# An encoder trunk of two layers: latent and neighbourhood attention heads in turns instead of one kind after the other

## The reference

```python
def even_mixer(h, w_in0, g_q, g_kv, w_uq, w_ukv, rpb, w_out0):
    u = h @ w_in0
    q_lat, kv_lat, k_rope, na_q, na_k, na_v, gate = jnp.split(u, ...)
    o_mla = mla(q_lat, kv_lat, k_rope, g_q, g_kv, w_uq, w_ukv)     # 8 heads, 512 x 512 scores each
    o_na = neighbourhood_attn(na_q, na_k, na_v, rpb)               # 8 heads, a window on an 8 x 64 grid, with a bias table
    o = jnp.concatenate([o_mla, o_na], axis=-1) * jax.nn.silu(gate)
    return o @ w_out0
```

## Time and profile before

| | |
|---|---|
| median of 3 runs | 1521.56 us (1518.37 to 1523.8) |
| profiled execution, device time | 1518.78 us |
| its span | 1517.0 us |
| PE busy | 1468.3 us (97%) |
| DVE busy | 849.7 us (56%) |
| ACT busy | 678.4 us (45%) |
| POOL busy | 345.4 us (23%) |

### The profile page before, as it was taken

One profiled execution on the slowest core, in us unless ns is written; L12 is line 12 of the kernel. 1 busy time (PEld: TensorE's weight loads), 2 busy tenths in 40 slices (PEclk: granted clock), 3 DMA queues, 4 the chain that ended last, 5 costly groups with the idle time before them and its releaser, 6 DMA issues.

```text
span 1517.0 us, 18952 instructions
## 1 busy us (share of the span) xinstructions
PE 1468.3 (97%) x7200; PEld 1119.7 (74%) x7200; DVE 849.7 (56%) x1523; ACT 678.4 (45%) x1170; POOL 345.4 (23%) x441
## 2 busy tenths in 40 slices
PE   8999999999999999999999999999999999999996
PEld 4777665678777787788887887567867778787885
DVE  4523345655887517785444345565688651789423
ACT  3323436654433435544544343674443353555333
POOL 0001123431200023765210002342120002376311
PEclk9999999999999999999999999999999999999998
DMA  9456742114232331116334443221432333111531
GB/s 383 157 203 221 248 154 98 50 54 144 91 94 85 117 118 52 47 28 236 91 93 157 131 114 117 84 56 57 139 97 84 98 108 115 57 42 29 181 97 69
DMA packets 54618, 174.27 MB, mean 115 GB/s; under 512 B 6000, under 2 KB 7408, under 8 KB 52224
## 3 DMA queue, kind: packets, MB, share of 16 engines
q1 hardware_dynamic: 54528, 173.07, 35.4%
HBM read 149.94 MB, written 23.10 MB: 114 GB/s over the span
## 4 chain that ended last, share of the span: by engine, by line
PE 81%; DVE 8%; ACT 5%; issue 2%; DMA 2%; POOL 1%; SPq 0%; DVEq 0%; ACTq 0%; POOLq 0%
PE ps L556 21%; PE ps L558 21%; PE ps L557 21%; PE ps L1098 3%; PE ps L1133 2%; PE ps L1152 2%; PE ps L302 2%; PE ps L1621 1%; PE ps L1604 1%; DVE w_lo L538 1%; PE ps L1655 1%; PE ps L1444 1%; PE ps L1115 1%; DMA at<-w_ada 1%; ACT w_hi L526 1%
## 5 line engine op out<-in xcount | busy, mean ns | idle before, releaser
L538 DVE TENSOR_TENSOR w_lo<-at,w_hi 128x1024 fp32r<-128x1024 f32 x160 | 200.5, 1253 | 355.2 <-ACT w_hi L526 355.1
L526 ACT ACTIVATE w_hi<-at 128x1024 fp32r<-128x1024 f32 x162 | 169.2, 1046 | 122.3 <-PE ps L558 122.3
L556 PE MATMUL ps<-h_e_hi,w_hi 128*128 128x512 f32 x480 | 190.9, 398 | 7.8 <-DVE w_lo L538 7.8
L558 PE MATMUL ps<-h_e_hi,w_lo 128*128 128x512 f32 x480 | 187.1, 390 | 0.0
L557 PE MATMUL ps<-h_e_lo,w_hi 128*128 128x512 f32 x480 | 186.9, 389 | 0.0
L556 PE MATMUL ps<-h_a_hi,w_hi 128*128 128x512 f32 x384 | 153.5, 400 | 1.8 <-DVE h_a_lo L588 1.0
L557 PE MATMUL ps<-h_a_lo,w_hi 128*128 128x512 f32 x384 | 150.3, 392 | 0.0
L558 PE MATMUL ps<-h_a_hi,w_lo 128*128 128x512 f32 x384 | 150.1, 391 | 0.0
L556 PEld LDWEIGHTS ps<-h_e_hi,w_hi 128*128 128x128 f32 x480 | 90.0, 188 | 43.6 <-DVE at L1430 11.7
L558 PEld LDWEIGHTS ps<-h_e_hi,w_lo 128*128 128x128 f32 x480 | 90.1, 188 | 19.4
L557 PEld LDWEIGHTS ps<-h_e_lo,w_hi 128*128 128x128 f32 x480 | 90.1, 188 | 18.3 <-issue 0.5
(11 more groups left out here) (291 smaller groups left out, 2967.3 us busy)
## 6 DMA issues: line engine op xcount, KB each, us to landing
at<-blocks_in SPq DMA_DIRECT2D x162, 512.0 KB, 3.7
at<-w_ada SPq DMA_DIRECT2D x32, 512.0 KB, 4.5
at<-w_ada SPq DMA_DIRECT2D x8, 1024.0 KB, 18.3
at<-xs SPq DMA_DIRECT2D x4, 2048.0 KB, 10.2
z_kept<-at SPq DMA_DIRECT2D x32, 256.0 KB, 2.2
at<-z_kept SPq DMA_DIRECT2D x32, 256.0 KB, 2.8
sg_kept<-at SPq DMA_DIRECT2D x16, 256.0 KB, 4.5
at<-sg_kept SPq DMA_DIRECT2D x16, 256.0 KB, 2.6
```

The source lines that it names most:

```text
L526: act.activation(whi[:, n % PAIRS, :, cols], wring[:, n % SLOTS, :, cols], ACT.Copy).then_inc(sem("w_hi"), 1)
L538: dve.tensor_tensor(wlo[:, n % PAIRS], wring[:, n % SLOTS], whi[:, n % PAIRS].bitcast(F32), ALU.subtract)\
L556: pe.matmul(o, stationary[0], moving[0], start=first, stop=False)
L558: return pe.matmul(o, stationary[1], moving[0], start=False, stop=final)
```

## The change

The order of the 24 steps becomes four times: four halves of two latent heads, then two neighbourhood heads. With q, r = divmod(j, 6), r = 0 to 3 are latent heads 2q and 2q+1 (halves 0, 0, 1, 1) and r = 4 and 5 neighbourhood heads 2q and 2q+1. The loop of each engine, its instructions and their number stay. What follows from it: the chunks of the output are gated in the order 0, 4, 1, 5, 2, 6, 3, 7 (`place`, `BY_PLACE`), latent ones from bank 6 and neighbourhood ones from bank 7; each quad product waits for the exponentials of step j-1; a latent score product two steps behind a neighbourhood step waits for the bias-and-maximum of that step, which is what reads its banks; the loads of tables and gate chunks on SP are put in a new order with new waits. The diff, cut to its core:

```diff
     def stats(j):
-        return slice(2 * j, 2 * j + 2) if j < 2 * HEADS else slice(4 * j - 4 * HEADS, 4 * j - 4 * HEADS + 4)
+        q, r = divmod(j, 6)
+        lo = 16 * q + (2 * r if r < 4 else 4 * r - 8)
+        return slice(lo, lo + (2 if r < 4 else 4))
...
         def attention_pair(j):
-            if j >= MLA_END:
-                return HEADS + j - MLA_END, 0
-            quad, e = divmod(j, 2)
-            return 2 * (quad // 2) + e, quad % 2
+            q, r = divmod(j, 6)
+            return (2 * q + r % 2, r // 2) if r < 4 else (HEADS + 2 * q + r - 4, 0)
+        def near(j):
+            return j % 6 >= 4
+        def place(c):
+            return 2 * (c % 4) + c // 4
+        BY_PLACE = (0, 4, 1, 5, 2, 6, 3, 7)
-        MLA_END = 2 * HEADS
-        GATED = (8, 12, 16, 20, 22, 24, 26, 28)
+        GATED = (8, 10, 14, 16, 20, 22, 26, 28)
...
         def c_sync(sp):
             def bias(h):
                 if h >= 3:
-                    sp.wait_ge(sem("c_max"), at("c_max", MLA_END + h - 2))
+                    sp.wait_ge(sem("c_max"), at("c_max", 6 * ((h - 3) // 2) + 5 + (h - 3) % 2))
...
-            for c in range(2, 5):
-                gate(c)
-            for h in range(3, 7):
-                bias(h)
-            gate(5)
-            bias(7)
-            gate(6)
+            bias(3)
+            bias(4)
+            gate(2)
+            gate(3)
+            for p in range(4, 7):
+                bias(p + 1)
+                gate(p)
             gate(7)
...
                 if j >= 2:
-                    pe.wait_ge(sem("c_exp"), at("c_exp", j - 1))
+                    free = "c_max" if near(j - 2) else "c_exp"
+                    pe.wait_ge(sem(free), at(free, j - 1))
...
-                if j == MLA_END:
-                    pe.wait_ge(sem("c_exp"), at("c_exp", j))
-                else:
-                    pe.wait_ge(sem("c_max"), at("c_max", j))
+                pe.wait_ge(sem("c_exp"), at("c_exp", j))
...
-                if half == 0 and n >= 2:
-                    pe.wait_ge(sem("d_tmp"), at("d_tmp", n - 1))
+                if half == 0 and place(n) >= 2:
+                    pe.wait_ge(sem("d_tmp"), at("d_tmp", place(n) - 1))
...
-                        last = pe.matmul(ps(6 + n % 2)[64 * e:64 * e + 64, 2 * P * half:2 * P * half + 2 * P],
+                        last = pe.matmul(ps(6 + n // 4)[64 * e:64 * e + 64, 2 * P * half:2 * P * half + 2 * P],
...
             for i in range(HALVES + LV):
-                if i < MLA_END:
+                if i < HALVES and not near(i):
                     score_pair(i)
...
-                    for k in range(3):
+                    for k in BY_PLACE[:3]:
                         out0(pe, 0, k)
...
-            for j, part in ((0, range(3, 7)), (1, range(3)), (0, (7,)), (1, range(3, DC))):
+            for j, part in ((0, BY_PLACE[3:7]), (1, BY_PLACE[:3]), (0, (7,)), (1, BY_PLACE[3:])):
```

More of the change, by code:

```diff
@@ L1042, in bias, with gate @@
                 if h >= 3:
-                    sp.wait_ge(sem("c_max"), at("c_max", MLA_END + h - 2))
+                    sp.wait_ge(sem("c_max"), at("c_max", 6 * ((h - 3) // 2) + 5 + (h - 3) % 2))
                 sp.dma_start(T2[:, h % 3], t2_masked[h]).then_inc(sem(f"t2_in{h % 3}"), 16)
[L1046 to L1049, removed]
+            def gate(p):
+                if p >= 2:
+                    sp.wait_ge(sem("d_tmp"), at("d_tmp", p - 1))
+                sp.dma_start(sg0[:, p % 2], sg_kept[BY_PLACE[p]]).then_inc(sem(f"sg_in{p % 2}"), 16)
             sp.wait_ge(sem("b_rs"), at("b_rs", 1))
@@ L1131, in turn @@
                             col = 2 * P * (s % 2) + P * e
-                            m, k = (e, s) if j < MLA_END else (NEAR[s][e][0] // 2, 2 * (NEAR[s][e][0] % 2) + NEAR[s][e][1])
+                            m, k = (e, s) if not near(j) else (NEAR[s][e][0] // 2, 2 * (NEAR[s][e][0] % 2) + NEAR[s][e][1])
                             last = pe.transpose(ps(4 + q)[:, col:col + P], Pt[:, j % 4, m, k * P:(k + 1) * P], ident)
@@ L1163, in near_values @@
                     for e in range(2):
-                        o = ps(6 + n % 2)[64 * e:64 * e + 64]
+                        o = ps(6 + n // 4)[64 * e:64 * e + 64]
                         w = nav[:, v, (2 * n + e) % HEADS]
@@ L1198, in lo_o @@
             def lo_o(c):
-                dve.wait_ge(sem("d_hi"), at("d_hi", c + 1))
-                dve.tensor_tensor(o_D[1][:, c], otmp[c % 2], o_D[0][:, c].bitcast(F32), ALU.subtract).then_inc(sem("d_o"), 1)
+                dve.wait_ge(sem("d_hi"), at("d_hi", place(c) + 1))
+                dve.tensor_tensor(o_D[1][:, c], otmp[c // 4], o_D[0][:, c].bitcast(F32), ALU.subtract).then_inc(sem("d_o"), 1)
             for i in range(HALVES + 7):
                 if i in GATED:
-                    c = GATED.index(i)
+                    p = GATED.index(i)
                     dve.wait_ge(sem("c_pv"), at("c_pv", i - LV))
-                    dve.wait_ge(sem(f"sg_in{c % 2}"), at(f"sg_in{c % 2}", 16 * (c // 2 + 1)))
-                    dve.tensor_tensor(otmp[c % 2], ps(6 + c % 2), sg0[:, c % 2], ALU.mult).then_inc(sem("d_tmp"), 1)
+                    dve.wait_ge(sem(f"sg_in{p % 2}"), at(f"sg_in{p % 2}", 16 * (p // 2 + 1)))
+                    dve.tensor_tensor(otmp[p % 2], ps(6 + p % 2), sg0[:, p % 2], ALU.mult).then_inc(sem("d_tmp"), 1)
                 if i - 2 in GATED:
-                    lo_o(GATED.index(i - 2))
+                    lo_o(BY_PLACE[GATED.index(i - 2)])
                 if i < HALVES:
@@ L1213, in c_vector @@
                     if u < HEADS:
-                        dve.tensor_reduce(nmx[:, 2 * i:2 * i + 2], ps2(i % 2).rearrange("p (e t) -> p e t", e=2), AX.X,
+                        dve.tensor_reduce(nmx[:, stats(i)], ps2(i % 2).rearrange("p (e t) -> p e t", e=2), AX.X,
                                           ALU.max, negate=True).then_inc(sem("c_max"), 1)
@@ L1240, in c_scalar @@
                 if i - 1 in GATED:
-                    c = GATED.index(i - 1)
-                    act.wait_ge(sem("d_tmp"), at("d_tmp", c + 1))
-                    act.activation(o_D[0][:, c], otmp[c % 2], ACT.Copy).then_inc(sem("d_hi"), 1)
+                    p = GATED.index(i - 1)
+                    act.wait_ge(sem("d_tmp"), at("d_tmp", p + 1))
+                    act.activation(o_D[0][:, BY_PLACE[p]], otmp[p % 2], ACT.Copy).then_inc(sem("d_hi"), 1)
                 if i < TM:
@@ L1264, in c_scalar @@
                         else:
-                            near = Pt[:, i % 4, m // 2, 2 * P * (m % 2):2 * P * (m % 2 + 1)]
-                            last = act.activation(near, near, ACT.Exp, bias=nmx[:, n:n + 1], scale=-1.0, accum_out=rsum[:, n:n + 1])
+                            part = Pt[:, i % 4, m // 2, 2 * P * (m % 2):2 * P * (m % 2 + 1)]
+                            last = act.activation(part, part, ACT.Exp, bias=nmx[:, n:n + 1], scale=-1.0, accum_out=rsum[:, n:n + 1])
                     last.then_inc(sem("c_exp"), 1)
@@ L1273, in c_gpsimd @@
                 pool.wait_ge(sem("c_ri"), at("c_ri", j + 1))
-                w = T if j < MLA_END else T // 2
+                w = T // 2 if near(j) else T
                 for m, n in enumerate(range(stats(j).start, stats(j).stop)):
@@ L1291, in out0 @@
             if j < 2:
-                pe.wait_ge(sem("d_o"), at("d_o", k + 1))
+                pe.wait_ge(sem("d_o"), at("d_o", place(k) + 1))
             last = three(pe, ps(j % 4), (whi[:, pair_of(b), k], wlo[:, pair_of(b), k]), (o_D[0][:, k], o_D[1][:, k]),
```

## The result

The changed kernel takes 1524.53 us, median of 8 runs (1522.03 to 1528.37). The kernel before, run beside it, takes 1519.69 (1518.11 to 1523.8). The ratio is 1.003, with a 95% interval of 1.0021 to 1.0038: +4.6 us, between 3.2 and 5.8. The forecast was +3.8 and 1525.4 us. So the kernel is slower by a little, as laid out, and the larger part of this text asks whether for the reasons given.

The account below looks back on a forecast made before the run. PE, busy for 97% of the span, was taken as the bound. Start wait, pairs, latent stretches and last pair gave +1.91 us per request, +3.8 for two, on a 1521.56 median: 1525.4 us, range 1517.5 to 1531.5.

Parts of the forecast that it names:

- The wait at the start: At i = 4 the first quad product waits for step 3's exponential on ScalarE: 1.80 us in each request.
- The seam's price for every pair: Old latent-to-neighbourhood transition, already mixed, takes 6.38 us a pair, 0.91 lost between turns; pairs at steps 4, 10, 16 cost that.
- rival A: Latent work fills the gaps between a neighbourhood pair's turns: -3.5 us, 1518.1; chance 0.10, 0.04 more without the start's wait.
- The four latent steps: Each stretch of four latent steps ending in a quad product takes 7.26 + 7.37 us on PE.
- The sum: PE's stage from i = 4 to 24: 71.24 us for 69.26, then -0.07; +1.91 per request, +3.8 for two.
- what I had costed at nothing: Eight side effects, among them table loads, new waits, gate products, rounding copies, normalisations and SBUF places: 0 us each.
- B: Bias tables land late and hold VectorE's step 4 and PE's turn of step 2: +7.8 us, 1529.4; chance 0.12.
- C: Exponential at r = 3 late, up to 0.6 us at three quads per request: +3.6 on top, 1529.0; chance 0.10.
- The clock: Granted clock stays 1.00; a lower one behind the 1.80 us wait would make the forecast wrong altogether.

Follow-up runs that it names:

- third kernel: Changed kernel with PE's turn ahead of the quad product and VectorE's copy ahead of its bias-and-maximum work, against the kernel before: 1522.99 us, ratio 1.0016.
- all-edits kernels: PE's turn, VectorE's and ScalarE's copies first, last-pair copies earlier, against the kernel before: 0.9996 (order of after), 1.0004 (order of before), 0.9971 (0 1 4 2 5 3 6 7).
- last kernel tried: Kernel before with only step 21's copies put ahead of the last exponential on ScalarE and the last reciprocal on VectorE: 1520.29 us, ratio 1.0004.
- fastest kernel: Head-pair order 0 1 4 2 5 3 6 7 (0 to 3 latent), turn and copies first, last-pair copies earlier, against the kernel before: 1515.42 us, ratio 0.9971.

## Why the prediction was right, and where it was off

**The wait at the start: right.** Worked out as 1.80 us with L1262 as the releaser; the timeline shows 1.80, and ScalarE's exponential (now L1269) as the releaser. The kernel with one early pair has it too and costs as much; the one with the first quad after eight latent steps has neither. So the cause of the loss is shown by two runs, and not only argued.

**The seam's price for every pair: right.** 6.38 worked out for a pair, 6.39 to 6.45 seen, with the waits of 0.34 and 0.20 to 0.23 in place. The seam in the trace of before was a sample of the new order, and it was the evidence against rival A.

**The four latent steps: right.** 14.63 worked out, 14.63 and 14.64 seen.

**The sum: right, a little small.** The stretch from i = 4 to 24 came to 71.34 against 71.24 worked out. Of the stage, the part up to the score product of step 6 grew by 1.04 in the first request of the undisturbed profile (the sum has 1.80 + 6.38 - 7.16 = 1.02), the part from there to i = 24 by 1.05 (the sum has 0.96), the rest by -0.06 (the sum has -0.07). Per request +2.03 for +1.91, in all +4.1 for +3.8. Of the 0.10 by which the stretch exceeds the sum, 0.04 lie in the last pair (6.45 for 6.41), 0.04 in the three pairs before it (19.18 for 19.14) and 0.02 in the three latent stretches (43.91 for 43.89); so what I had costed at nothing did cost nothing. The interval of the ratio's +4.6 (3.2 to 5.8) holds both sums.

**The time itself: closer than the sum had earned.** The 1525.4 stood on three runs of the kernel before with a median of 1521.56; over eight it is 1519.69. The baseline was 1.9 too high and the change 1.0 too low (medians 4.8 apart for 3.8), and these two errors have opposite signs. That the forecast missed by only 0.9 us is in part luck. The range was also not what its sentence says: half of the scatter of 2.7, put on top of 1518.1 and 1529, gives about 1516.7 to 1530.4, and not 1517.5 to 1531.5. The measured time lies well within either.

**Rival A, the mix fills the gaps: did not happen.** PE's idle time rose from 2.27 to 3.88 us. But it was not impossible. With the order inside a pair changed, the pair falls to 5.57, and the mixed order 0 1 4 2 5 3 6 7 then gives 0.9971, where the order of before with the same edits gives 1.0004 (the stages without a fall: 90.14 against 91.69, 1.55 us per request). The waits fit that: in the order of before PE waits for ScalarE between the pairs (0.91, 0.29 and 0.42 us), in the mixed one once (0.90). The Trainium skill (Perfetto Trace Analysis, Optimization Strategy) says that performance may be improved by interleaving regimes in which the most-contended engine changes. Here PE is the busiest engine in both stretches (43.54 of 43.58 us, 23.46 of 25.68), so the case fits it only loosely, and the mix paid only in that last form: the idle time came from the order of the copies within a pair, and no neighbour could fill it until that was changed.

**Rivals B and C: did not happen.** The waits of after in the second request (engine and line, releaser: us in all, times, longest; those of the first are the same):

```profile
PEld ps L1122 <- ACT at L1269: 2.6, 4, 1.9
DVE at L1230 <- PE ps L1122: 3.8, 4, 2.7
```

VectorE's bias work L1230 waits for the quad product alone, in both requests, and never for a DMA, so the tables came in time. The quads' weight loads wait 2.6 us in four times, of which 1.9 is the start; the other three share 0.7, 0.23 each, and so stay under the 0.5 that I had set for C.

**The clock: not in the sum, and half open.** I said that a lower granted clock behind the 1.80 wait would make the forecast wrong. It was 1.00 behind that wait in every profile. It fell elsewhere: behind the gap of 2.1 to 2.4 us at the start of the second request's stage, in seven of the thirteen profiles (five of the six whose order has an early pair, and two of the seven others, one of these with the heads in the order of before). So it comes with the old order too, and without fail with neither. Such a fall made the stage longer by 0.8 to 2.5 us, so some more of them in the changed kernel would explain the half microsecond between +4.1 and +4.6. The mean granted clock was 0.9929 over 15 executions of the changed kernel and 0.9937 over 82 of the kernel before; among the latter 0.001 less goes with about 0.7 us more, so by this estimate the difference is worth 0.6 us. But the kernel with one early pair had 0.9938 in five executions and cost as much. The half microsecond may as well be scatter, being less than the interval. Whether the new order makes such falls more frequent was not settled.

**Where my expectations of the experiments fell.** From the third kernel on I summed the shorter pairs and took the end of the stage to stay. The step that failed is "what is late next": the chain from the last quad through VectorE's maximum, ScalarE's exponentials of steps 22 and 23, the copy or GpSimd's normalisation, to PE's turn. It doesn't get shorter when PE is early. Saved time came back there as waits of 1.9 to 2.5 us, and behind some of these the clock fell, which took about 1.5 us more (3.54 for 2.01). How the distance between the all-edits kernels in the orders of after and 0 1 4 2 5 3 6 7 (3.2 us) divides between start wait, a wait of 2.06 and the clock was not tried apart.

## What to carry to other kernels

Before moving two kinds of work together, look for a place where the old order has them side by side already, and take its rhythm from the trace: it is the price of the mix. Ask of every stage's first steps whether the buffer that a larger product takes is already free: here the chain through the exponentials was hidden at step 8 and bare at step 4. When a wait in the middle is removed, lay out the end of the stage as well, for PE that arrives early only waits there unless the last copies and exponentials are put in the order in which they are needed. And try the mix again once the gap's own cause is gone: with the same edits, the mixed order 0 1 4 2 5 3 6 7 was faster than the old one by 1.55 us per request, where the full mix gained nothing that could be told apart.

## What the runs showed of the hardware

In these profiles the granted clock can halve behind a gap of 1.6 to 2.5 us in the work of PE, and need not. Before and after have nearly the same gap, 2.15 and 2.19 us: no fall in the one, a fall in the other. The shortest single gap with a fall behind it is 1.56 us, at the start of the first request's stage in the last kernel tried; in the twelve other profiles the gap at that place is 1.34 to 1.56 us, and none has a fall. PE's timeline and the windows behind it:

```profile
228.99 1.99 PE L1103 MATMUL ps<-at,at 96*128 96x512 f32 x4 [1.56 <-DVE at L982]
```

```profile
231.00:234.00 3.00, 3.00 (x7) 2.09 (x7) 1.22 (x1) 2.18 (x5) 0.00 (x0) 0.50 0.00 0
```

In one execution of one kernel a wait of 1.94 us was followed by 24 products in 3.54 us in the first request and in 2.01 in the second. Behind the waits of 0.90 and 1.47 us of the fastest kernel, and behind the new 1.80 at the start, no profile shows one. What decides was not found. A fall is seen in the duration of instructions and in the windows' clock, and not in idle time: the busy time of PE rises instead (1469.8 and 1471.2 us in the two profiles of the changed kernel, without and with a fall in the stage), which reads like more work if one doesn't look at the clock.

The time of a whole execution goes with its mean granted clock. Over 82 executions of the kernel before, those with 0.995 took 1517.93 to 1520.33 us, and those with 0.990 took 1522.77 to 1523.04. A difference of 0.3% between two kernels is of the size of a few such falls, so it takes the ratio of several runs, and a stage time from a profile without a fall, to tell an order's cost from the clock's.
